# A two-layer decoder trunk: key/value modulation multiplied in the first attention's tail, a seventh ring slot, and 32-column strips for experts of at most 32 tokens

## The reference, cut to what matters

```python
def grouped_moe(h, router_w, router_b, w_gate, w_up, w_down):
    probs = softmax(t @ router_w); sel = probs + router_b
    # best group of four experts, then the best two in it; their gates add up to 1
    for e in range(N_EXPERTS):
        a = silu(t @ w_gate[e]) * (t @ w_up[e])        # 1024 -> 512
        out = out + gates[:, e:e + 1] * (a @ w_down[e])  # 512 -> 1024
# per layer: x = norm(alpha*x + (1+g_a)*attention(modulate(x))); x = norm(alpha*x + (1+g_f)*grouped_moe(modulate(x)))
```

## Time and profile before

| | us |
|---|---|
| median of 3 runs | 900.73 (900.71 to 902.5) |
| the profiled execution: span | 899.3 |
| TensorE busy in it | 834.7 (93%) |
| VectorE, ScalarE, GpSimd busy | 376.0, 127.1, 90.3 |
| read from HBM | 302.49 MB, 338 GB/s over the span |

### The profile page before, as it was taken

One profiled execution on the slowest core, in us unless ns is written; L12 is line 12 of the kernel. 1 busy time (PEld: TensorE's weight loads), 2 busy tenths in 40 slices (PEclk: granted clock), 3 DMA queues, 4 the chain that ended last, 5 costly groups with the idle time before them and its releaser, 6 DMA issues.

```text
span 899.3 us, 10792 instructions
## 1 busy us (share of the span) xinstructions
PE 834.7 (93%) x3730; PEld 393.0 (44%) x3730; DVE 376.0 (42%) x927; ACT 127.1 (14%) x341; POOL 90.3 (10%) x146
## 2 busy tenths in 40 slices
PE   6899999999998998899979999999999999889984
PEld 3584675435333333333328557654533333333331
DVE  2185867475211221222148688828521122212215
ACT  1001243011100000000010114611110000010010
POOL 1000000051110001011004000215111110000000
PEclk9999999999999999999999999999999999999998
DMA  8999982019999999999999799405499999999901
GB/s 352 431 421 426 399 329 95 1 59 431 426 428 426 425 427 426 427 426 426 425 384 419 299 426 425 175 0 213 163 406 424 428 424 427 426 427 426 392 12 47
DMA packets 23408, 304.59 MB, mean 339 GB/s; under 512 B 2720, under 2 KB 3232, under 8 KB 5280
## 3 DMA queue, kind: packets, MB, share of 16 engines
q1 hardware_dynamic: 22752, 303.14, 80.6%
q10 hardware_dynamic: 576, 0.40, 0.1%
HBM read 302.49 MB, written 1.05 MB: 338 GB/s over the span
## 4 chain that ended last, share of the span: by engine, by line
PE 68%; DMA 21%; DVE 8%; issue 2%; POOL 1%; ACT 1%; POOLq 0%; DVEq 0%; ACTq 0%
PE ps L1724 17%; DMA ring<-in_moe_w_up_dram 12%; PE ps L1732 7%; PE ps L1558 6%; PE ps L1529 6%; PE ps L1542 6%; PE ps L1642 5%; PE ps L1737 4%; DMA stream<-in_moe_w_up_dram 3%; DMA ring<-in_ada_w_dram 3%; DMA ring<-in_moe_w_down_dram 3%; PE ps L1453 1%; PE ps L1431 1%; PE ps L1705 1%; PE ps L1465 1%
## 5 line engine op out<-in xcount | busy, mean ns | idle before, releaser
L1724 PE MATMUL ps<-ring,hT 128*64 128x512 f32 x384 | 172.4, 599 | 11.8 <-DMA ring<-in_moe_w_up_dram 9.9
L1725 PE MATMUL ps<-ring,hT 128*64 128x512 f32 x384 | 172.7, 600 | 0.0
L1233 DVE TENSOR_TENSOR arena<-arena,ps 128x256 f32<-128x256 f32 x32 | 13.5, 421 | 233.8 <-ACT arena L802 126.8
L1724 PEld LDWEIGHTS ps<-ring,hT 128*64 128x64 f32 x384 | 51.1, 138 | 117.4 <-issue 117.4
L1732 PE MATMUL ps<-ring,arena 128*64 128x512 f32 x208 | 94.8, 599 | 0.0
L1733 PE MATMUL ps<-ring,arena 128*64 128x512 f32 x208 | 94.8, 598 | 0.0
L414 DVE SCALAR_TENSOR_TENSOR spare<-ring,csig,spare 128x512 f32<-128x512 f32 x112 | 86.1, 769 | 3.8
L1737 PE MATMUL ps<-arena 128*128 128x512 f32 x144 | 66.6, 605 | 3.2 <-DVE arena L1242 3.2
L1724 PE MATMUL ps<-spare,hT 128*64 128x512 f32 x128 | 58.9, 609 | 2.7 <-DMA stream<-in_moe_w_up_dram 2.5
L1725 PE MATMUL ps<-stream,hT 128*64 128x512 f32 x128 | 58.9, 610 | 0.0
L1529 PE MATMUL ps<-hT,ring 128*128 128x256 f32 x256 | 57.2, 386 | 1.5 <-ACT hT L680 1.5
(11 more groups left out here) (281 smaller groups left out, 1083.3 us busy)
## 6 DMA issues: line engine op xcount, KB each, us to landing
ring<-in_moe_w_down_dram SPq DMA_DIRECT2D x26, 2048.0 KB, 21.8
ring<-in_ada_w_dram SPq DMA_DIRECT2D x24, 2048.0 KB, 14.7
ring<-in_moe_w_gate_dram SPq DMA_DIRECT2D x24, 2048.0 KB, 18.4
ring<-in_moe_w_up_dram SPq DMA_DIRECT2D x24, 2048.0 KB, 21.3
spare<-in_moe_w_gate_dram SPq DMA_DIRECT2D x8, 2048.0 KB, 23.2
stream<-in_moe_w_up_dram SPq DMA_DIRECT2D x8, 2048.0 KB, 25.3
ring<-in_fox_w_in_dram SPq DMA_DIRECT2D x6, 2048.0 KB, 9.8
ring<-in_kv_ada_w_dram SPq DMA_DIRECT2D x4, 2048.0 KB, 13.8
```

Of the source, the lines that this page charges most:

```text
L1724: t.matmul(ps[0:CAP, bank, :], lhs(k), wcols(ng)[:, k, :], start=(k == 0), stop=(k == KC - 1))
L1725: mm = t.matmul(ps[CAP:P, bank, :], lhs(k), wcols(nu)[:, k, :], start=(k == 0), stop=(k == KC - 1))
```

## The change

Three things, and what goes with them. `mod_product(3)` moves into bank 7 and into the first attention's tail, in four parts of two steps; `turn_mod` and `mod_cols` follow behind the second gate's, and `zeroed` takes the places left. The ring has seven slots; to make room, the router's tables are put into the arena and the reserve for dynamic DMAs is set to 1024 bytes. An expert of at most 32 tokens is computed by the four-strip routines, chosen on TensorE by a branch on a new table `tabl`; the two halves of its sums are added by four products with `folded` (128 columns) in the place of the four transposes. To give it one order of work for both kinds, a pair is no longer interleaved but done expert by expert, and VectorE, not GpSimd, cuts out the overflow windows. `put_pair` makes 8 products of 32 columns for a pair, not 4 of 64.

```diff
-RING = 6
+RING = 7
-            return {2: 6, 3: 0}.get(gi, 7)
+            return {2: 6}.get(gi, 7)
@@ GpSimd, windows @@
-                def overflow(i, j):
...
                 def window(i, j, o):
-                    if i:
-                        spent(pool, N_MOE[l] + 6 * (i - 1) + 2 * j + 1)
+                    if i or l:
+                        pool.wait_ge(gu_mm[j], i + 8 * l)
@@ ScalarE, experts and program @@
-                    overflow(i, 0)
-                    spent(act, n0 + 1)
+                    act.wait_ge(gu_mm[0], q + 1)
                     a.activation(gu[:, 0, :], ps[:, 4, :], ACT.Copy).then_inc(gu_ev[0], 1)
+                    overflow(i, 0)
                     act.wait_ge(tg_mm[0], q + 1)
...
+            mod_row_out(3)
             turned(1)
             router_exp(0)
-            mod_row_out(3)
             experts(0)
@@ VectorE, route @@
-                if l == 0:
-                    mod_cols(3, 5)
...
+                totals, past = rt[:, 7, 0:NE], rt[:, 7, NE:2 * NE]
+                link(d.tensor_tensor(totals, each[:, 0:NE], each[:, NE:2 * NE], ALU.add))
+                link(d.tensor_scalar(past, totals, float(OCAP), float(OCAP), ALU.is_gt, ALU.mult))
+                link(d.tensor_tensor(t3(2), pos[:, :, 0:NE], past.unsqueeze(1).broadcast_to([P, NB, NE]), ALU.subtract))
+                link(d.tensor_copy(tabl[:, :], past[0:1, :]))
...
-                tot = cnt[:, 1, :]
-                link(d.tensor_tensor(tot, each[0:1, 0:NE], each[0:1, NE:2 * NE], ALU.add))
+                tot = totals[0:1, :]
@@ VectorE, experts and program @@
                     overflow(i, 0)
                     put_pair(i)
                     glu(0, q)
+                    dve.wait_ge(sc_mm, i + (10 * l + 1))
+                    spent(dve, n0 + 4)
+                    gated(y, 0, 4, y_ev[0])
                     overflow(i, 1)
-                    glu(1, q)
-                    dve.wait_ge(sc_mm, i + (10 * l + 1))
                     dve.wait_ge(tp_mm, q + 1)
                     d.tensor_copy(putT[:, :], ps[:, 6, 0:S]).then_inc(tp_ev, 1)
-                    spent(dve, n0 + 4)
-                    gated(y, 0, 4, y_ev[0])
+                    glu(1, q)
                     spent(dve, n0 + 5)
                     gated(y, CAP, 5, y_ev[1])
...
             mod_cols(2, 4)
             gate_row(1, 5)
+            mod_cols(3, 7)
             fold_cols(1)
             post_norm(0)
@@ TensorE, experts @@
+                def between(i, j, q, n0):
+
+                    if j == 0:
+                        pe.wait_ge(tp_ev, q + 1)
+                        pe.wait_ge(y_ev[1], (q + 1) * 2)
+                        add_back(0, 0, putT, y).then_inc(used[slot(n0)], 1)
+                        add_back(0, 1, putT, y).then_inc(used[slot(n0 + 1)], 1)
+                    else:
+                        pe.wait_ge(putted, (q + 1) * 8)
+                        for b in range(NB):
+                            mm = t.transpose(ps[:, 6, b * P:(b + 1) * P], put[:, b, :], ident[:, :])
+                            if b == 0:
+                                mm.then_inc(used[slot(n0 + 2)], 1)
+                        mm.then_inc(tp_mm, 1)
+                    pe.wait_ge(gu_ev[j], q + 1)
+
+                def ahead_of_down(i, j, q, n0):
+
+                    if j == 0:
+                        add_back(1, 0, putT, y)
+                        add_back(1, 1, putT, y).then_inc(sc_mm, 1)
+                    pe.wait_ge(at_r[j], q + 1)
+                    landed(pe, n0 + 4 + j)
...
+                    for j in range(2):
+                        pe.wait_ge(y_ev[j], (q + 1) * 2)
+                        landed(pe, n0 + 2 * j)
+                        landed(pe, n0 + 2 * j + 1)
+                        pe.wait_ge(xw_r[j], q + 1)
+                        large = pe.value_load(tabl[0:1, bass.ds(i * 2 + j, 1)], min_val=0, max_val=OCAP)
+                        with pe.If(large > 0):
+                            gate_up(i, j, lambda k: xw[:, j, k, 0:CAP], 4 + j, range(KC)).then_inc(gu_mm[j], 1)
+                            overflow(i, j)
+                            between(i, j, q, n0)
...
+                            ahead_of_down(i, j, q, n0)
+                            down(i, j, lambda f: aT[:, j, f * CAP:(f + 1) * CAP], 4 + j).then_inc(used[slot(n0 + 4 + j)], 1)
+                        with pe.Else():
+                            gate_up_strips(i, j, xw[:, j, :, :], 4 + j).then_inc(gu_mm[j], 1)
+                            between(i, j, q, n0)
+                            for f in range(4):
+                                mm = t.matmul(ps[:, 4 + j, f * P:(f + 1) * P], gu[:, j, f * P:(f + 1) * P], folded,
+                                              start=True, stop=True)
...
+                            ahead_of_down(i, j, q, n0)
+                            down_strips(i, j, aT[:, j, :].rearrange("p (c s) -> p c s", c=4), 4 + j
+                                        ).then_inc(used[slot(n0 + 4 + j)], 1)
@@ TensorE, program @@
+                if p == PAIRS_H - 1:
+                    pe.wait_ge(q_ev, PAIRS_H)
+                    mod_product(3, range(0, 2))
                 if p >= 2:
                     for T in (2 * p - 4, 2 * p - 3):
                         turn_probs(T, T % 4, 2 * (T + 1))
...
             fox_values(PAIRS_H - 3)
+            mod_product(3, range(2, 4))
             for T in (HF - 2, HF - 1):
                 turn_probs(T, T % 4, 2 * (T + 1))
...
             out_part(0, 1, 0, range(0, 4))
+            mod_product(3, range(4, 6))
             fox_values(PAIRS_H - 1)
+            mod_product(3, range(6, KC))
             out_weights(0, 4)
...
             spread_gate(1, 5)
+            turn_mod(3, 7)
```

More of the change, by code:

```diff
@@ L638, in pair @@
                         window(i, j, starts[j])
-                    for j in range(2):
-                        overflow(i, j)
                 pool.wait_ge(tab, l + 1)
@@ L1494, in turn_stream @@
                 for b in range(NB):
-                    if b and norm == 0:
-                        mod_product(3, range(0, 2))
                     if b and norm == 1:
                         mod_product(4, range(5, KC))
-                    if b and norm == 2:
+                    elif b:
                         zeroed((0, 1, 0))
@@ L1658, in route @@
                 m = (1, 4)[l]
-                if l == 0:
-                    mod_product(3, range(2, 4))
-                else:
-                    zeroed((0, 1))
+                zeroed((0, 1))
                 stream_turned(m)
@@ L1812, in experts @@
-                    mm.then_inc(tg_mm[0], 1)
-                    gate_up(i, 1, lambda k: xw[:, 1, k, 0:CAP], 5, range(4, KC))
-                    overflow(i, 1)
-                    add_back(0, 0, putT, y).then_inc(used[slot(n0 + 2)], 1)
-                    add_back(0, 1, putT, y).then_inc(used[slot(n0 + 3)], 1)
-                    add_back(1, 0, putT, y)
-                    add_back(1, 1, putT, y).then_inc(sc_mm, 1)
-                    pe.wait_ge(gu_ev[1], q + 1)
-                    for f in range(4):
-                        mm = t.transpose(ps[:, 5, f * P:(f + 1) * P], gu[:, 1, f * P:(f + 1) * P], ident[:, :])
@@ L1822, in experts @@
-                    mm.then_inc(tg_mm[1], 1)
-                    pe.wait_ge(at_r[0], q + 1)
-                    landed(pe, n0 + 4)
-                    down(i, 0, lambda f: aT[:, 0, f * CAP:(f + 1) * CAP], 4).then_inc(used[slot(n0 + 4)], 1)
-                    pe.wait_ge(putted, (q + 1) * 4)
-                    for b in range(NB):
-                        mm = t.transpose(ps[:, 6, b * P:(b + 1) * P], put[:, b, :], ident[:, :])
-                    mm.then_inc(tp_mm, 1)
-                    pe.wait_ge(at_r[1], q + 1)
```

131 lines of the change are left out of this document (58 added, 73 removed).

## The result

The changed kernel is **slower**: 907.8 us median of 20 runs, against 901.05 of the kernel before beside it; ratio 1.0067, 95% interval 1.0051 to 1.0082. The forecast was 884. So it is 0.7% slower, little, but clear of the noise. The profiled execution took 908.86 us and has a span of 907.1 (899.3 before), so 1.8 us lie around it.

A forecast was written before the change was run, and what follows sets the result against it. The start of the loads was taken to bound the first expert stage, TensorE the second. 899.3 - 15.0 (first layer) - 2.3 (second) = 882, with 1.4 around the span 883.5, taken as 884; range 877 to 893, chance 0.70.

The forecast's parts named there:

- the price of the branch: TensorE's new register read and branch per expert: 0.5 us taken, between 0 and 1.81 us.
- the 4 us to spare: First layer: experts done at 441.5, the loads of group 4 land last at 445.5, by 4 us.
- overflow's body is jumped today without a gap: Argument against a dear branch: TensorE already jumps over the overflow body, with no gap shown.
- the branch is dear: Rival: read, branch and target fetch cost 2.6 us an expert, 2.1 above the 0.5; 909 us, slower; chance 0.09.
- The clock: Rival: TensorE's clock falls at every expert, seven counting in either layer; 900 us, no change; chance 0.10.
- The 1.4 us for a fall: TensorE's clock dropping to 1.2 GHz after a long wait: 1.4 us a fall, one priced in the second layer.
- Part 1 and part 2: Tail costs 5.5 us; piece 8 issued at 221.8, experts at 222.7; group 4 lands at 445.5, 15.0 us earlier.
- Part 3's sums: TensorE time per expert: large 14.5 us (j = 0) or 14.2 (j = 1), small 10.2 or 9.4.
- 8 us of branches in the second layer: TensorE's register reads and branches in the second expert stage: 8 us of the 237.3 summed.
- 18 were summed: TensorE's waits for down pieces: some 9 us in the first layer, some 9 in the second.
- The 1.4 us around the span: Time of the execution outside the profiled span: 1.4 us, added to 882 and taken for the median too.
- the 17.3 us that it summed up: Whole gain on the span: 15.0 us in the first layer, 2.3 in the second, from 899.3 to 882.

The follow-up runs named there:

- experiment 7: Experiment 4's seven-slot kernel plus, ahead of each expert pair, a jump over a never-run body of 0 to 256 products; 906.49 and 939.07 us, one run each.
- experiment 2: The changed kernel with the two arms of the branch exchanged, small expert's arm first; 905.31 us, ratio 1.0104.
- experiment 8: Experiment 4's seven-slot kernel plus a 128-product jump, three times under busy DMA engines and twice in the quiet second attention's end; 901.99 us, one run.
- experiment 4: Kernel before with parts 1 and 2 alone, pairs interleaved, 64 columns for all; 882.36 us with seven slots (0.9818), 889.19 with six (0.9894).
- experiment 6: Expert pieces loaded in order of use: with experiment 1's static choice 882.94 us (0.979), with three short branches per expert 888.9 (0.9851).
- experiment 1: The changed kernel with each expert's arm picked at build time from known counts, no branch over an arm; 884.13 us, ratio 0.984.
- experiment 9: Parts 1 and 2, pairs interleaved, strips for small experts chosen by short branches around each product group; 883.44 us, ratio 0.9826.
- the first measurement: Experiment 7's first run: jumps over bodies of 0, 1, 8, 16, 32, 48, 64 and 128 products, reversed in the second layer; 906.49 us.
- the second measurement: Experiment 7's second run: jumps over bodies of 0, 56, 64, 72, 80, 96, 112 and 256 products, reversed in the second layer; 939.07 us.

## Why the prediction was wrong

- **The failed step** is the price of the branch: "I take 0.5", between 0 and 1.81 us an expert. Measured, it is 47.2 / 18 = 2.6 us for a small expert and nothing for a large one, plus a low clock behind most stops: TensorE waits for the fetch of instructions behind the long arm. So TensorE, not the loads, ends the first layer's experts, and the 4 us to spare that the forecast had there are gone. The reason given against more, "overflow's body is jumped today without a gap", is true of 34 products and was carried to 65. The two lie on either side of what experiment 7 shows, nothing up to 48 and up to 5.6 us from 56 on.
- **The rival "the branch is dear"** was the right one: 909 told, 907.8 measured. Its 2.6 us were taken from a transfer's time and for all experts alike; only the small ones pay, in stops of 2 to 5.3 us and a low clock. The mechanism was right, a fetch; that the total fits to 1.2 us is luck. The Trainium skill (Runtime: NRT & Kernel Launch, section "Instruction fetch mechanics") was weighed there, with its stall for a target that is not yet held; experiments 2, 7 and 8 agree with it, and it should have had more than 0.09.
- **The clock** is no rival of its own: the gaps of 1.38 us at j = 1 mostly leave it alone (249.19 above, 1.92 for down), the long stops mostly make it fall. The 1.4 us for a fall was right in kind: mostly 1.3 to 1.7 on strips, 2.3 to 2.7 on twelve steps of 64 columns.
- **Part 1 and part 2** were right in the main: piece 8 at 221.81 (221.8), experts at 222.46 without the branch (222.7), group 4 at 445.74 where TensorE is ready for it (445.5). The last fits partly by luck: that execution issues piece 1 at 164.68, 2.9 us ahead of experiment 4's (167.55), and in experiment 6, with 167.32, group 4 is there at 448.22. So the loads gain some 12 to 13 us in the first layer, not 15.0. Six slots give 1.1% of the 1.8%.
- **Part 3's sums** for one expert were right within 0.8 us: in experiment 1 a small j = 0 takes 230.09 - 220.26 = 9.8 (10.2), a small j = 1 8.6 (9.4); above, a large j = 0 takes 290.83 - 276.16 = 14.7 (14.5). Without the branch the time is 884.1, the forecast's 884, and that is luck too: the forecast held 8 us of branches in the second layer that this kernel has not, while TensorE waits 25.5 us for down pieces where 18 were summed, and the first layer gains 3 us less. The 1.4 us around the span were the difference of two executions; in one and the same they are 1.7 (883.9 and 882.2 in experiment 1).
- **What the forecast had but did not say**: 15.0 of the 17.3 us that it summed up came from parts 1 and 2. It valued the whole and never asked what each part was worth alone. Measured, parts 1 and 2 by themselves shorten the span by 18.6 us, 6.7 of them in the second stage, where the forecast had 2.3 with part 3; so part 3 would have stood there with a gain near nothing, since small experts wait for loads in both stages, and a risk of 25 us.

## What to carry to other kernels

A single branch around a long unrolled body is priced by the products jumped over: here nothing up to 48, up to 5.6 us from 56 on, and behind the longer stops a fall of the clock, while the weights stream at 425 GB/s. Choose when the program is built where that is allowed; else keep the jumped body short, but keep the branches few as well, since many short ones cost 44.5 us of stops in experiment 9. And when a change has several parts, value each against the bound that the others leave: work taken from TensorE is worth little where it then waits for loads.

## What the runs showed of the hardware

- A jump over much program costs a time that does not grow with its length: 112 to 256 products all cost 3.9 to 5.6 us while the weights stream, and each of these stops ends 1.4 to 1.6 us after an instruction packet has landed.
- The program jumped over is mostly loaded too: the 594 products never run in the first measurement raise the packets of the instruction queue q8 from 47 to 56, 66 products a packet of 16.4 KB. The 1472 of the second raise it to 65 only, 82 products a packet, so of its longest bodies a part is not loaded. The queue's rows in the first and the second measurement (packets, MB, share):

```profile
q8 instruction: 56, 0.92, 0.4%
```

```profile
q8 instruction: 65, 1.06, 0.4%
```

By the Trainium skill (Runtime: NRT & Kernel Launch, section "Instruction fetch mechanics") instructions come in blocks of 16 KiB, 256 of them. A packet of the first measurement is as large; by my estimate from its 66 products a packet, a product then is some four instructions. It gives TensorE a store of 2048 instructions, eight blocks, and speaks of a window of two pages for the target of a branch. Here a jump over 64 products, by this estimate some 256 instructions, can stop TensorE and one over 112, some 450, always did under load: that fits one to two blocks ready ahead, not eight.

- The fetch is slower beside the weights: the same jump over 128 products shows 4.9 to 5.2 us at some 420 GB/s and 0 to 0.43 where the DMA engines are nearly idle (3 to 10 GB/s), two places in one run.
- A register read and branch that no queued products cover costs TensorE about 1 us: 1.7 to 2.3 us of standing still ahead of the first expert of a layer with them, 0.95 to 0.97 without.
